# Feed-forward up projection: one product of 512 columns per block of high weights, halves added outside TensorE

## The reference, cut to what matters

```python
h2 = rms_norm(x, norm_ffn[l])
up = causal_dwconv(h2 @ w_up[l], ffn_conv_w[l], ffn_conv_b[l])   # w_up: 1024 x 6144, 3 taps per channel
gate_h, val_h = jnp.split(up, 2, axis=-1)
x = x + (jax.nn.gelu(gate_h, approximate=True) * val_h) @ w_down[l]
```

## Time and profile before

| | us |
|---|---|
| median of 3 runs (lowest, highest) | 1577.75 (1576.43, 1579.17) |
| the profiled execution, its own time | 1575.39 |
| its span (first to last instruction) | 1573.3 |
| PE busy | 1559.8 |
| DVE / ACT / POOL busy | 1070.1 / 880.9 / 883.9 |
| up stage, first `ffn_scale` to last | 1373.7 to 1498.7 |
| first matmul of the down projection | 1498.4 |

### The profile page before, as it was taken

How to read it: one execution, slowest core, us unless ns; L and a number is a source line. 1 busy time by engine, 2 the same in 40 slices (tenths; PEclk the granted TensorE clock), 3 DMA queues, 4 the chain that set the end, 5 groups by cost and what they waited for, 6 DMA issues and landing times.

```text
span 1573.3 us, 33476 instructions
## 1 busy us (share of the span) xinstructions
PE 1559.8 (99%) x12568; PEld 1471.2 (94%) x12568; DVE 1070.1 (68%) x1867; ACT 880.9 (56%) x1251; POOL 883.9 (56%) x413
## 2 busy tenths in 40 slices
PE   9999999999999999999999999999999999999998
PEld 8999899999999999998888888889999999999998
DVE  7998743879933777778888766676937484455522
ACT  6566765554454444444444445557677654676653
POOL 8786468968886000000000244457876689898886
PEclk9999999999999999999999999999999999999999
DMA  6564335555555555555555665556543356565553
GB/s 223 171 197 157 107 123 188 192 183 190 191 183 196 176 163 183 173 167 170 185 177 170 218 195 193 196 200 189 173 143 107 118 170 190 192 199 188 189 196 124
DMA packets 86217, 277.03 MB, mean 176 GB/s; under 512 B 11232, under 2 KB 18160, under 8 KB 86128
## 3 DMA queue, kind: packets, MB, share of 16 engines
q1 hardware_dynamic: 85712, 274.76, 53.7%
q0 software_dynamic: 272, 1.05, 0.2%
q10 hardware_dynamic: 144, 0.00, 0.0%
HBM read 274.73 MB, written 1.05 MB: 175 GB/s over the span
## 4 chain that ended last, share of the span: by engine, by line
PE 92%; issue 2%; DVE 2%; POOL 2%; ACT 2%; DMA 0%; SPq 0%; DVEq 0%; ACTq 0%; POOLq 0%
PE gemm L679 35%; PE gemm L996 22%; PE gemm L698 18%; PE aux L1282 4%; PE gemm L827 3%; PE aux L976 2%; POOL w_lo L466 1%; PE gemm L714 1%; PE gemm L739 1%; ACT w_hi L1378 1%; PE gemm L1282 1%; PE aux L946 0%; PE gemm L813 0%; PE gemm L720 0%; PE gemm L756 0%
## 5 line engine op out<-in xcount | busy, mean ns | idle before, releaser
L466 POOL TENSOR_TENSOR w_lo<-raw,w_hi 128x1024 fp32r<-128x1024 f32 (+1 forms) x330 | 789.8, 2402 | 279.9 <-ACT w_hi L1378 275.8
L1378 ACT ACTIVATE w_hi<-raw 128x1024 fp32r<-128x1024 f32 (+1 forms) x492 | 514.7, 1048 | 556.8 <-PE gemm L679 310.4
L679 PE MATMUL gemm<-h_lo,w_hi 128*128 128x256 f32 x2144 | 504.7, 277 | 0.0
L679 PE MATMUL gemm<-h_hi,w_hi 128*128 128x256 f32 x2096 | 499.8, 279 | 1.1 <-ACT w_hi L1378 1.0
L679 PEld LDWEIGHTS gemm<-h_lo,w_hi 128*128 128x128 f32 x2144 | 402.8, 188 | 0.7 <-issue 0.2
L679 PEld LDWEIGHTS gemm<-h_hi,w_hi 128*128 128x128 f32 x2096 | 394.3, 188 | 3.8 <-issue 1.6
L698 PE MATMUL gemm<-h_hi,w_lo 128*128 128x256 f32 x2096 | 284.6, 277 | 2.4 <-POOL w_lo L466 1.5
L698 PEld LDWEIGHTS gemm<-h_hi,w_lo 128*128 128x128 f32 x2096 | 259.8, 188 | 4.9 <-POOL w_lo L466 3.4
L466 DVE TENSOR_TENSOR w_lo<-raw,w_hi 128x1024 fp32r<-128x1024 f32 x162 | 195.5, 1221 | 100.6 <-ACT w_hi L1378 99.5
L996 PE MATMUL gemm<-w_hi,act_parts 128*128 128x512 f32 x1008 | 247.9, 386 | 0.4 <-ACT act_parts L1579 0.4
L996 PEld LDWEIGHTS gemm<-w_hi,act_parts 128*128 128x128 f32 x1008 | 187.6, 187 | 36.6 <-issue 0.5
(11 more groups left out here) (436 smaller groups left out, 2175.9 us busy)
## 6 DMA issues: line engine op xcount, KB each, us to landing
raw<-in_w_u SPq DMA_DIRECT2D x128, 512.0 KB, 3.5
raw<-in_w_ev SPq DMA_DIRECT2D x128, 512.0 KB, 3.6
raw<-in_w_up SPq DMA_DIRECT2D x48, 512.0 KB, 3.5
raw<-in_w_gate SPq DMA_DIRECT2D x24, 512.0 KB, 3.8
raw<-in_w_down SPq DMA_DIRECT2D x24, 512.0 KB, 3.5
raw<-in_w_conv_in SPq DMA_DIRECT2D x16, 512.0 KB, 4.3
raw<-in_w_peer_q SPq DMA_DIRECT2D x16, 512.0 KB, 3.8
raw<-in_w_branch SPq DMA_DIRECT2D x24, 288.0 KB, 2.8
```

The lines of the kernel that those rows point to most:

```text
L466: eng.tensor_tensor(w_lo[v][:, 0:n], raw[c.raw][v][:, 0:n], w_hi[v][:, 0:n], ALU.subtract).then_inc(lo_ready[v], 1)
L679: return pe.matmul(spread(out), w[:, k, :], spread(x[n][:, k, :]), start=(n == k == 0), stop=False)
L1378: act.activation(w_hi[v][:, 0:n], raw[c.raw][v][:, 0:n], ACT.Copy).then_inc(hi_ready[v], 1)
```

## The change

For chunks 1 to 23 of the up stage the two inputs lie side by side in one tile `ffn_h` (high part, low part: 512 columns), and each block of high weights is multiplied with both in one matmul. The two tiles of a chunk now take a whole bank each: columns 0 to 255 hold hi·hi, columns 256 to 511 hi·lo plus lo·hi. A chunk takes two of the four banks, so TensorE needs a chunk's banks again two chunks later. The two halves are added outside: ScalarE copies the upper half of both banks into a new SBUF tile `up_sum` (`ffn_low_sums`, queued ahead of the last tap), and VectorE adds the lower halves to it. The scaling and the taps then work on `up_sum` in SBUF, not on the bank in PSUM. The banks are free after VectorE's additions. Chunk 0 stays a `paced_product` in one bank; VectorE copies it into `up_sum`. Elsewhere three semaphores of the first block are merged into one (same instructions, same order).

```diff
+            def wide_product(s, it):
+                c = plan["up"][s]
+                if s >= 2:
+                    pe.wait_ge(evacuated[plan["up"][s - 2].bank], it + plan["up"][s - 2].bank_use)
...
+                for v in range(2):
+                    bank = up_bank(s, v)
+                    pe.wait_ge(hi_ready[v], it * BANKS + (c.split + 1))
+                    w = by_k(w_hi[v], P)
+                    for k in range(KD):
+                        mm = pe.matmul(spread(bank[:, :]), w[:, k, :],
+                                       spread(ffn_h[:, k].rearrange("p n t -> p (n t)")), start=(k == 0), stop=False,
+                                       skip_group_check=True)
+                    mm.then_inc(hi_used[v], 1)
+                    pe.wait_ge(lo_ready[v], it * BANKS + (c.split + 1))
+                    w = by_k(w_lo[v], P)
+                    for k in range(KD):
+                        mm = pe.matmul(spread(bank[:, T:2 * T]), w[:, k, :], spread(ffn_h[:, k, 0, :]), start=False,
+                                       stop=(k == KD - 1), skip_group_check=True)
+                    mm.then_inc(tile_done[v], 1)
...
-                    act.activation(uc[:, b, v, :], pair(gemm[c.bank])[:, v, :], ACT.Identity,
+                    act.activation(uc[:, b, v, :], up_sum[:, b, v, :], ACT.Identity,
...
+            def ffn_low_sums(s, n, it=0):
+                if not isinstance(n, int) or n >= 2:
+                    act.wait_ge(ffn_tapped, n - 1)
+                for v in range(2):
+                    act.wait_ge(tile_done[v], it * BANKS + (plan["up"][s].index + 1))
+                    ins = act.activation(up_sum[:, s % 2, v, :], up_bank(s, v)[:, T:2 * T], ACT.Copy)
+                ins.then_inc(ffn_lows, 1)
...
                     ffn_round((s + 1) % 2, n - 1)
+                    ffn_low_sums(s, n, it)
                 ffn_last_tap(c, s % 2, n, it)
...
             def ffn_scale(s, n, it=0):
                 c = plan["up"][s]
-                taken(dve, c, it)
-                bank = pair(gemm[c.bank])
-                dve.tensor_tensor(bank, bank, both, ALU.mult).then_inc(ffn_scaled, 1)
+                b = s % 2
+                if isinstance(n, int) and n == 0:
+                    taken(dve, c)
+                    dve.tensor_copy(up_sum[:, b], pair(gemm[c.bank])).then_inc(evacuated[c.bank], 1)
+                else:
+                    dve.wait_ge(ffn_lows, n)
+                    for v in range(2):
+                        ins = dve.tensor_tensor(up_sum[:, b, v, :], up_sum[:, b, v, :], up_bank(s, v)[:, 0:T], ALU.add)
+                    ins.then_inc(evacuated[c.bank], 1)
+                dve.wait_ge(evacuated[c.bank], it + c.bank_use)
+                dve.tensor_tensor(up_sum[:, b], up_sum[:, b], both, ALU.mult).then_inc(ffn_scaled, 1)
...
-                        ins = dve.scalar_tensor_tensor(uc[:, b, v, back:], pair(gemm[c.bank])[:, v, 0:T - back], tap,
+                        ins = dve.scalar_tensor_tensor(uc[:, b, v, back:], up_sum[:, b, v, 0:T - back], tap,
                                                        uc[:, b, v, back:], ALU.mult, ALU.add)
```

More of the change, by code:

```diff
@@ L191, in build @@
         sb("ahead_of_h", [P, 8])
+        with nc.sbuf_tensor("ffn_h", [P, KD, 2, T], F32R) as ffn_h:
+            pass
+        ffn_parts = (ffn_h[:, :, 0, :], ffn_h[:, :, 1, :])
         h_hi = sb("h_hi", [P, KD, T], F32R)
@@ L362, in build @@
         uc = carve(2, 2, T)
+        carve = carver(big, AT_M)
+        up_sum = carve(2, 2, T)
         ffg, ffp = [[aux[n + b][:, 0:T] for b in range(2)] for n in (0, 2)]
@@ L382, in build @@
          y_rounded, y_split, ob_rounded, ob_split,
-         dve_step, f_abs, f_exp, f_soft, c_ready, sel_ready, conv_summed, conv_moved, conv_done, mean_ready, centered,
+         dve_step, ffn_tapped, ffn_lows, f_soft, c_ready, sel_ready, conv_summed, conv_moved, conv_done, mean_ready, centered,
          ln_squared, ln_paired, ln_sumsq, ln_std, ln_scaled, ln_sig, conv_act, gates_on,
@@ L388, in build @@
              "y_rounded y_split ob_rounded ob_split "
-             "dve_step f_abs f_exp f_soft c_ready sel_ready conv_summed conv_moved conv_done mean_ready centered "
+             "dve_step ffn_tapped ffn_lows f_soft c_ready sel_ready conv_summed conv_moved conv_done mean_ready centered "
              "ln_squared ln_paired ln_sumsq ln_std ln_scaled ln_sig conv_act gates_on "
@@ L434, in spread, with up_bank @@
             return tile.rearrange("p (j g c) -> p g j c", g=4, c=4)
+        def up_bank(s, v):
+            return gemm[(plan["up"][0].bank + 2 * (s % 2) + v) % BANKS]
         def by_k(tile, m, rows=P, n=KD):
@@ L661, in product @@
                     product_tile(c, v, m, it, x, steps)
+            def wide_product(s, it):
+                c = plan["up"][s]
+                if s >= 2:
+                    pe.wait_ge(evacuated[plan["up"][s - 2].bank], it + plan["up"][s - 2].bank_use)
+                elif not isinstance(it, int):
+                    pe.wait_ge(evacuated[plan["up"][s + 2].bank], it + (plan["up"][s + 2].bank_use - 1))
+                for v in range(2):
[13 more added lines that the diff above has]
+                    mm.then_inc(tile_done[v], 1)
             def bank_free(c, it=None):
@@ L1262, in _ @@
                 product(c, P, x=m_parts)
-            paced_product(plan["up"][0], P, h_rounded, h_split, 4 * OPEN_UP)
+            paced_product(plan["up"][0], P, h_rounded, h_split, 4 * OPEN_UP, ffn_parts)
             sum_gathered(5)
-            for c in plan["up"][1:BANKS]:
-                product(c, P)
+            moved(pe, plan["out2"])
+            for s in range(1, BANKS):
+                wide_product(s, 0)
             with pe.Fori(1, KF // BANKS) as it:
-                for c in plan["up"][:BANKS]:
-                    product(c, P, it)
+                for s in range(BANKS):
+                    wide_product(s, it)
             for i, c in enumerate(plan["down"]):
@@ L1456, in _ @@
                     moved(act, plan["f"])
-                    act.activation(fa, fy, ACT.Abs).then_inc(f_abs, 1)
-                    act.wait_ge(f_abs, 1)
-                    act.activation(fe, fa, ACT.Exp, scale=-1.0).then_inc(f_exp, 1)
+                    act.activation(fa, fy, ACT.Abs).then_inc(f_soft, 1)
+                    act.wait_ge(f_soft, 1)
+                    act.activation(fe, fa, ACT.Exp, scale=-1.0).then_inc(f_soft, 1)
                 if i == 1:
-                    act.wait_ge(f_exp, 1)
+                    act.wait_ge(f_soft, 2)
                     act.activation(fl, fe, ACT.Ln, bias=1.0).then_inc(f_soft, 1)
@@ L1848, in _ @@
                 act.activation(x_hi[:, part, :], pair(aux[i]), ACT.Copy).then_inc(m_rounded, 1)
-            gained_pairs("out2", OPEN_UP, "norm_ffn_2", h_hi, sq)
+            gained_pairs("out2", OPEN_UP, "norm_ffn_2", ffn_parts[0], sq)
             def ffn_column(name, v, n, per=1, w=0):
@@ L2072, in _ @@
             moved(dve, plan["f"])
-            dve.wait_ge(f_soft, 1)
+            dve.wait_ge(f_soft, 3)
             step(dve.scalar_tensor_tensor(fa, fy, 0.0, fl, ALU.min, ALU.subtract))
@@ L2603, in _ @@
             merged_rest(3)
-            open_residual("out2", 5, OPEN_UP, (h_hi, h_lo), sq)
+            open_residual("out2", 5, OPEN_UP, ffn_parts, sq)
             invert_deviation(5)
@@ L2630, in ffn_convolve @@
                         else:
-                            ins.then_inc(evacuated[c.bank], 1)
+                            ins.then_inc(ffn_tapped, 1)
             def ffn_multiply(s, n, it=0):
-                b, c = s % 2, plan["up"][s]
-                dve.wait_ge(evacuated[c.bank], it + c.bank_use)
+                b = s % 2
+                dve.wait_ge(ffn_tapped, n + 1)
                 dve.wait_ge(ffn_gelu, n + 1)
```

## The result

The changed kernel takes 1645.01 us (median of 5, 1643.79 to 1647.11) against 1577.75 before: a ratio of 1.0427, 95% interval 1.0415 to 1.0438. It is 67.3 us slower; 1648 was forecast. Its profiled execution took 1645.06, with a span of 1643.3 against 1573.3.

A forecast was written before the change was run, and what follows sets the result against it. The prediction took TensorE as the bound before, and after the change an ACT-DVE loop blocked by GpSimd: chunk 0, 22 periods of 8.4 us and the way out gave +70.3 us, 1648 as median; range 1598 to 1676.

The forecast's parts named there:

- The saving on TensorE: Up stage: 16 wide matmuls replace 32 per chunk, saving 0.1 us per chunk, 2.3 us over 23 chunks.
- The loop: Up stage, scaling to scaling through ACT and DVE with new copies and additions: 6.5 us undisturbed, 8.4 with GpSimd's blocking.
- The signs: Profile marks named beforehand: scaling period 8 to 9.5 us, high matmuls 223 ns apart, PE idle, ACT's last tap waiting 1.9 or more.
- The blocking: Up stage: DVE scaling and taps with two SBUF inputs and GpSimd's subtractions block each other by whole instructions; period 8.4 us.
- The order of turns: Up stage: GpSimd's tile 0 subtraction goes after DVE's third tap and before the fourth; period 8.4 us.
- the other order: Up stage: DVE's fourth tap goes before GpSimd's subtraction, and the scaling waits for both subtractions; period 8.1 us, total 1641.
- the third order: Up stage: GpSimd's subtraction goes ahead of DVE's third tap, and the scaling waits for the second subtraction; 9.45 us, total 1671.
- The sum: Whole kernel: chunk 0's scaling ends at 1376.0, 22 periods of 8.4, then the way out; +70.3 us, median 1648.
- The way out: Entry to the down projection: from chunk 22's scaling at 1560.8 to TensorE through two chunks at 1579.8, against 1509.5 before.
- Only the round trip: Rival, up stage: blocking does not hold for these operations, loop 6.5 us, total 1601; chance 0.15.
- TensorE still the bound: Rival, up stage: loop stays under TensorE's 5.4 us per chunk, −2.3 us, 1575, no change; chance 0.04.
- The clock: Rival, up stage: idle TensorE loses clock, period bounded at 10.8 us, total 1701; chance 0.05, shared with a worse order.

The follow-up runs named there:

- narrow matmuls: The changed kernel with each matmul of 512 columns split again into two of 256, into the same halves of the same banks: 1645.22 us, ratio 1.0429.
- the kernels without blocking: The changed kernel with sum, scaling and taps back in the PSUM bank: 1599.01 us; and with GpSimd subtracting only 64 of 1024 columns per tile: 1603.44 us.
- VectorE's in-bank version: The changed kernel without ScalarE's copies; VectorE copies the upper halves to SBUF, then adds, scales and taps in the bank: 1587.43 us, ratio 1.0059.
- The same kernel: The changed kernel with upper halves left out, no copies or additions, scaling from PSUM into SBUF, taps with two SBUF inputs, measured twice: 1613.89 and 1602.15 us.

## Why the prediction was right

**The saving on TensorE**: right in kind, and right that it is worth nothing where another loop is longer (narrow matmuls: no change). The term of 2.3 us was taken from matmuls of another stage; in the kernel without the sum the periods give 1.6, and the medians 2.3 with an interval that holds both.

**The loop**: right step by step. From the end of one scaling (1459.93) in the changed kernel, forecast in brackets: last taps end 1.33 (1.14), next rounding ends 2.28 (2.10), GpSimd starts 2.44 (2.25), the product gate x value ends 5.75 (5.58), the activation is rounded at 6.26 (6.15), copies end 6.82 (6.71), additions 7.60 (7.65), the scaling 8.33 (8.4). The late 0.2 comes with the last taps: their two instructions from SBUF take 1.09, where the row that I used had 0.91. The two copies and the additions took 0.66 and 0.75 (0.64 and 0.78). The signs came as named, but for one: ACT's last tap waited 1.75 for DVE, where 1.9 or more was named.

**The blocking**: right. Without it the loop is 6.49 with the taps on the bank and 6.51 with the taps on SBUF (forecast 6.5). The order of turns was the one that the times gave: the third tap ahead, the fourth behind, 2.60 us long. The price of the other order was wrong: with the fourth tap first the period would be 8.1, the lower bound, but the experiment measured 8.57, of which 0.15 is the handoff that its wait adds. The 9.45 of the third order was seen in no run.

**The sum**: 22 periods took 182.2 us (184.8): from 1378.04, the end of the first scaling, which lasted 1.56 as forecast by the earlier trace rows, to 1560.19. The steady period is 8.33 and three early ones are 7.9. The spans differ by 70.0, of which 2.1 arise ahead of the up stage: VectorE's reciprocal there starts at 1371.89 in one profile and 1373.97 in the other, and over the profiles of the experiments at 1372.0 to 1376.4. That is scatter of the part that is not changed.

**The way out** was right in its sum only. I had TensorE start the down projection 2.2 us after the scaling of chunk 22 and then wait for weights of the second chunk, 19.0 in all. What I left out is a wait in the program: the first down product waits for `ffn_act`, the product gate x value of chunk 22. TensorE, and its windows (PE busy, PEld, DVE, ACT, POOL, PEclk):

```profile
1565.96 2.07 PE L1315 MATMUL aux<-f_hi,w_hi 128*128 128x256 f32 x8 [5.11 <-DVE aux L2689]
1567.84 1.91 PE L1315 MATMUL aux<-f_lo,w_hi 128*128 128x256 f32 x8
```

```profile
1565.00:1568.00 3.00, 2.04 (x9) 2.04 (x10) 1.83 (x5) 0.94 (x3) 2.66 (x2) 0.50 0.53 167
```

It started 5.8 after that scaling, having stood for 5.1 us, and then ran at half the clock, 1.2 of 2.4 GHz. It was through two chunks at 1579.50, 19.3 after the scaling. So it started 3.6 us later than forecast and lost 2.5 more at half clock (its first three passes took 1571.25 − 1565.96 = 5.29, and the three that followed 2.76), and the 5.8 us of waits for weights that I had counted did not come, because the late start let the weights be there. That these errors cancel to 0.3 us is luck.

**The rivals.** Only the round trip: it is the time of the kernels without blocking, 1599 and 1603, not of this one. TensorE still the bound: it would have needed the copies, additions and scaling to take 1.1 us less; VectorE's in-bank version shows the nearest approach, with a period of 5.95. The clock: in the profile it did fall once inside the loop, behind a gap of 1.79 us, and it cost nothing. Window (columns as in the earlier trace rows) and TensorE there:

```profile
1510.00:1520.00 10.00, 7.95 (x38) 6.48 (x36) 6.50 (x12) 5.67 (x11) 5.09 (x2) 0.83 0.43 138
1512.44 3.07 PE L684 MATMUL gemm<-ffn_h,w_hi 128*128 128x512 f32 x8 [1.79 <-ACT w_hi L1411]
1515.30 1.72 PE L691 MATMUL gemm<-ffn_h,w_lo 128*128 128x256 f32 x8
```

The wide pass took 3.07 in place of 2.03 and the wait of 0.70 for `w_lo` was gone; the scalings on both sides are 1517.74 − 1509.41 = 8.33 apart as ever. With ScalarE's copies made twice, where TensorE's gaps reach 2.4 us, the granted clock averages 0.93 from 1380 to 1560, and from the fifth on the periods still are 8.9 to 9.0. So the clock did fall, as the rival has it, but rarely, and what it took was TensorE's slack.

## What to carry to other kernels

Halving the number of matmuls at the same number of streamed columns saves only what each matmul costs beyond its columns, here about 4 ns of 230; work that out from two rows before paying for it elsewhere. Slack in an in-order queue is not a sum: add the new instructions to the loop through all engines and compare that with the bound, since 1.4 us of new work did not fit into 1.8 us of waits. And where an operand moves from PSUM to SBUF, look at who else reads SBUF at that time: an operation with two SBUF inputs waits for a GpSimd instruction to end, and a free engine then waits with it.

## What the runs showed of the hardware

- VectorE and GpSimd take turns by whole instructions when both read two SBUF tensors. A tap of 0.47 us lasted 2.60 beside a subtraction of 2.4 and 0.54 beside one cut to 64 columns. The Trainium skill (SBUF — State Buffer, "Who interferes with whom") states the blocking; the trace agrees.
- The order of turns can keep itself up. The same kernel had periods of 6.57 and 7.06 us, and its executions fell into two groups, 1600 to 1603 and 1613 to 1615. In the pair of profiles a short fall of TensorE's clock near the start of the stage is where they part. Four executions could not have told the two groups from scatter.
- With gaps of 1.7 and 0.7 us in each period of 8.3, TensorE's granted clock was full but for one fall (0.83 from 1510 to 1520); with gaps of up to 2.4 it averaged 0.93 over the stage; behind one gap of 5.1 it was 0.50. In the loop the falls changed no period; behind the gap of 5.1 the half clock cost 2.5 us.
- ScalarE's scaled copy of 256 columns took 593 ns from SBUF in this stage against 561 from PSUM (last taps after and before).
